# Expert pairs in twelve half phases instead of six, and the pair with the largest second expert moved from fourth to second

## The reference

```python
D_MODEL = 1024; N_EXPERTS = 8; TOP_K = 2; D_FF_EXPERT = 3584
logits = xt @ w_router + b_router
top_p, top_e = lax.top_k(softmax(logits), TOP_K)      # weights normalised to sum 1
# every expert e, for the tokens that chose it:
ye = (silu(xe @ w_gate[e]) * (xe @ w_up[e])) @ w_down[e]
# and the sum of ye * p goes back to the token's row
```

## Time and profile before

| what | value |
|---|---|
| median of 3 runs | 1355.91 us (1355.67 to 1359.97) |
| profiled execution | 1356.35 us, span 1354.6 us |
| PE busy | 1285.1 us, 95% of the span |
| expert part, first gather to last scatter | 466.39 to about 1337.7 us |
| weights over the whole program | 458.94 MB read |

### The profile page before, as it was taken

How to read it: one execution, slowest core, us unless ns; L and a number is a source line. 1 busy time by engine, 2 the same in 40 slices (tenths; PEclk the granted TensorE clock), 3 DMA queues, 4 the chain that set the end, 5 groups by cost and what they waited for, 6 DMA issues and landing times.

```text
span 1354.6 us, 28860 instructions
## 1 busy us (share of the span) xinstructions
PE 1285.1 (95%) x12945; PEld 754.5 (56%) x12946; DVE 214.9 (16%) x592; ACT 125.4 (9%) x249; POOL 19.4 (1%) x107
## 2 busy tenths in 40 slices
PE   6999999999999699999899989799999899999996
PEld 3777788877886533346533336443435466643564
DVE  0298200000005401000101000021000020101002
ACT  2200310000002310000010000010000010000002
POOL 1000000000002000000000000000000000000000
PEclk8999999999999799999999999999999999999998
DMA  9999467656436689999999999999999997799992
GB/s 332 408 403 386 163 249 238 219 177 230 166 110 250 253 302 416 419 420 421 421 419 416 418 421 420 422 418 411 418 420 422 420 398 283 266 420 357 424 397 98
DMA packets 87886, 462.25 MB, mean 341 GB/s; under 512 B 8747, under 2 KB 12119, under 8 KB 52663
## 3 DMA queue, kind: packets, MB, share of 16 engines
q1 hardware_dynamic: 86257, 458.59, 85.4%
q10 hardware_dynamic: 1494, 1.67, 0.4%
HBM read 458.94 MB, written 2.24 MB: 340 GB/s over the span
## 4 chain that ended last, share of the span: by engine, by line
PE 84%; DMA 10%; issue 2%; DVE 2%; ACT 1%; POOL 1%; SPq 0%; DVEq 0%; ACTq 0%; POOLq 0%
PE bank L1640 34%; PE bank L1378 25%; PE bank L1666 14%; DMA ring<-in_w_exp_down_dram 10%; PE bank L1569 2%; PE bank L1347 2%; PE bank L1693 1%; PE bank L1592 1%; PE bank L1335 1%; PE bank L1276 1%; PE bank L1500 0%; DVE xT L936 0%; ACT MIX L869 0%; PE bank L1514 0%; PE bank L1327 0%
## 5 line engine op out<-in xcount | busy, mean ns | idle before, releaser
L1640 PE MATMUL bank<-ring,HT 128*32 128x384 f32 (+1 forms) x5376 | 510.6, 540 | 3.6 <-DMA ring<-in_w_exp_up_dram 3.6
L1640 PEld LDWEIGHTS bank<-ring,HT 128*32 128x32 f32 x5376 | 193.1, 110 | 309.1 <-issue 267.8
L1378 PE MATMUL bank<-HT,ring 128*128 128x264 f32 x1024 | 232.9, 389 | 2.5 <-POOL HT L610 2.5
L1378 PEld LDWEIGHTS bank<-HT,ring 128*128 128x128 f32 x1024 | 194.6, 191 | 44.0 <-issue 11.1
L1666 PE MATMUL bank<-ring,hid_t 128*32 128x256 f32 x2560 | 147.8, 379 | 1.3 <-DMA ring<-in_w_exp_down_dram 1.3
L1666 PEld LDWEIGHTS bank<-ring,hid_t 128*32 128x32 f32 x2560 | 85.2, 110 | 55.7 <-issue 4.3
L1378 PE MATMUL bank<-BIG,ring 128*128 128x264 f32 x480 | 108.0, 386 | 0.0
L1666 PE MATMUL bank<-ring,COND 128*32 128x256 f32 x1568 | 91.3, 385 | 16.0 <-DMA ring<-in_w_exp_down_dram 16.0
L1378 PEld LDWEIGHTS bank<-BIG,ring 128*128 128x128 f32 x480 | 91.1, 190 | 15.5
L1211 DVE TENSOR_TENSOR MIX<-bank,MIX 128x512 f32<-128x512 f32 (+1 forms) x42 | 26.2, 625 | 399.4 <-PE bank L1640 397.6
L1666 PEld LDWEIGHTS bank<-ring,COND 128*32 128x32 f32 x1568 | 49.5, 111 | 57.1 <-DMA ring<-in_w_exp_down_dram 26.0
(11 more groups left out here) (216 smaller groups left out, 489.8 us busy)
## 6 DMA issues: line engine op xcount, KB each, us to landing
ring<-in_w_exp_gate_dram SPq DMA_DIRECT2D x64, 1024.0 KB, 22.8
ring<-in_w_exp_up_dram SPq DMA_DIRECT2D x64, 1024.0 KB, 21.5
ring<-in_w_exp_down_dram SPq DMA_DIRECT2D x64, 1024.0 KB, 26.0
ring<-in_w_ada_dram SPq DMA_DIRECT2D x48, 1024.0 KB, 11.9
ring<-in_w_exp_gate_dram SPq DMA_DIRECT2D x64, 768.0 KB, 11.7
ring<-in_w_exp_up_dram SPq DMA_DIRECT2D x64, 768.0 KB, 15.2
ring<-in_w_exp_down_dram SPq DMA_DIRECT2D x32, 1536.0 KB, 28.0
ring<-in_w_in_dram SPq DMA_DIRECT2D x10, 1024.0 KB, 25.1
```

The source lines that it names most:

```text
L1378: ins = t_.matmul(banks_of[label][:, 0:NT], w[:, k, f * P:(f + 1) * P], src(k0 + k), start=(k0 + k == 0), stop=(k0 + k == k_tiles - 1))
L1640: ins = t_.matmul(bank[banks[g]][i * GRP:(i + 1) * GRP, 0:cols], xg[:, k, c0:c0 + GRP], w[:, i, :], start=(k == 0), stop=(k == DT - 1))
```

## The change

The order of the four pairs is now ranks (0, 4), (1, 7), (2, 5), (3, 6). A pair has twelve phases instead of six: gate large, gate small, up large, up small for the first half, the same for the other half, then down large and down small for each half. Gate and up of a group now share one bank, and silu is written straight to `hidT`, in place of the buffer `sil`. SP reads the second expert's number ahead of load 8 of pair 0 (it was load 16). The tables are issued by ACT, ahead of its first wait for `flags_ready`. PE waits for bank 7 after it has read the number of passes, not before.

```diff
-RANK_AT = (0, 4, 2, 5, 3, 6, 1, 7)
+RANK_AT = (0, 4, 1, 7, 2, 5, 3, 6)
-PHASES = (("large", 0), ("small", 1), ("large", 1), ("small", 0), ("large", "down"), ("small", "down"))
+PHASES = tuple((role, kind, HALVES[role][f])
+               for kind, f in (("gate", 0), ("up", 0), ("gate", 1), ("up", 1), ("down", 0), ("down", 1)) for role in ROLES)
+DOWN_LOADS = (range(0, 8), range(8, DOWN_UNITS))
...
-                    if first and start <= RING * UNIT < start + size:
-                        spread_tables()
-                    if first and n == 2 * DT:
+                    if first and n == DT:
                         sp.wait_ge(on("flags_ready"), 1)
                         experts.append(expert_at(1))
...
-                            a.activation(sil[:, g, 0:cols], bank[GATE_BANKS[role][g]][:, 0:cols],
+                            a.activation(hidT[role, half][g], bank[GATE_BANKS[role][g]][:, 0:cols],
                                          ACT.Silu).then_inc(on(f"{role}_silu"), step_of(g, n, most))
...
+            act.wait_ge(on("pmT_ready"), 1)
+            act.dma_start(pm_rows, pmT[:]).then_inc(on("pm_rows_stored"), 16)
+            act.wait_ge(on("pm_rows_stored"), 16)
+            for i, dst in enumerate((posb, wgtb)):
+                spread = pm_rows[i * NE:(i + 1) * NE, :].rearrange("e n -> (e n)").unsqueeze(0)
+                act.dma_start(dst.rearrange("p e n -> p (e n)"),
+                              spread.to_broadcast([P, NE * NT])).then_inc(on("tables_spread"), 16)
             act.wait_ge(on("flags_ready"), 1)
...
-            for bk in range(8):
+            for bk in range(7):
                 pe.wait_ge(emptied[bk], bank_total[bk])
             pe.wait_ge(on("flags_ready"), 1)
             passes = pe.value_load(flag[0:1, 2 * NE:2 * NE + 1], min_val=1, max_val=2)
+            pe.wait_ge(emptied[7], bank_total[7])
...
-                expand("large", 0, {})
-                expand("small", 0, {3: [("large", 0, g) for g in large[:3]], 5: [("large", 0, g) for g in large[3:]]})
-                expand("large", 1, {3: small[:count["small"]]})
-                expand("small", 1, {3: [("large", 1, g) for g in large[:3]], 5: [("large", 1, g) for g in large[3:]]})
-                down("large", {4: small[count["small"]:]})
-                down("small", {})
+                early, late = (4, 7) if count["small"] == 1 else (3, 5)
+                for s in range(2):
+                    large = [("large", s, g) for g in range(count["large"])]
+                    before_it = [("small", s - 1, g) for g in range(count["small"])] if s else []
+                    expand("large", "gate", s, {3: before_it})
+                    expand("small", "gate", s, {})
+                    expand("large", "up", s, {})
+                    expand("small", "up", s, {early: large[:3], late: large[3:]})
+                down("large", 0, {4: [("small", 1, g) for g in range(count["small"])]})
+                down("small", 0, {})
+                down("large", 1, {})
+                down("small", 1, {})
```

More of the change, by code:

```diff
@@ L103, in pair_loads @@
     starts, at = [], 0
[L104 to L109, removed]
+    for role, kind, half in PHASES:
+        for i in DOWN_LOADS[half] if kind == "down" else range(DT):
+            size = DOWN_PARTS[i] * D if kind == "down" else QUAD * SPLIT[half][1]
+            starts.append((role, kind if kind == "down" else f"{kind}{half}", i, at, size))
+            at += size
     assert at % (RING * UNIT) == 0 and len(starts) == PAIR_LOADS
@@ L503, in pair_units @@
                     end = start + size
-                    if (role, kind, i) == ("large", "up1", DT - 1):
+                    if n + 1 < PAIR_LOADS and LOADS[n + 1][:3] == ("small", "gate0", 0):
                         end += LOADS[n + 1][4]
@@ L1595, in bank_free @@
                 def bank_free(role, kind, s, g):
[L1596 to L1621, removed]
-                    else:
[L1623 to L1626, removed]
@@ L1628, in expand @@
-                def expand(role, s, turns):
-                    cols, groups = SPLIT[HALVES[role][s]][1], count[role]
[L1630 to L1648, removed]
@@ L1650, in down @@
-                def down(role, turns):
-                    groups, most = count[role], MOST[role]
-                    pe.wait_ge(on(f"{role}_hidT"), p * 2 * most + 2 * most)
[L1653 to L1657, removed]
+                    most = MOST[role]
+                    if kind == "up":
+                        pe.wait_ge(on(f"{role}_silu"), p * 2 * most + (s * most + g + 1))
+                    elif s:
+                        pe.wait_ge(on(f"{role}_hidT"), p * 2 * most + (g + 1))
+                    elif role == "small":
+                        pe.wait_ge(on("x_updated"), p * DT + DT)
+                    elif g < 4:
+                        pe.wait_ge(on("xg_ready"), p * 4 + (g + 1))
+                    else:
+                        pe.wait_ge(on("x_updated"), p * DT + 5)
@@ L1658, in down @@
+                def down(role, s, turns):
+                    groups, most, half = count[role], MOST[role], HALVES[role][s]
+                    pe.wait_ge(on(f"{role}_hidT"), p * 2 * most + 2 * most)
+                    for u in DOWN_LOADS[half]:
+                        for turned in turns.get(u, ()):
+                            turn_hid(*turned)
                         parts = DOWN_PARTS[u]
                         n, w = load(parts)
+                        first, last = u == DOWN_LOADS[half][0] and not s, u == DOWN_LOADS[half][-1] and s
```

59 lines of the change are left out of this document (31 added, 28 removed).

## The result

The changed kernel takes **1348.46 us** (median of 9 runs, 1345.37 to 1349.73); the kernel before, on the same chip, 1355.91. The ratio is 0.9934, 95% interval 0.9920 to 0.9947: 9 us less (7 to 11); the medians alone differ by 7.5. The forecast was 1345.8, with 1339 to 1355 as its range. The profiled execution took 1349.01 us, its span 1347.3.

The account below looks back on a forecast made before the run. Narrow pairs were taken as load-bound at 418 GB/s, the slim one as PE-bound, coupled by the ring. Last down matmul at 1322.0 plus an unchanged 24.3 us gave 1346.2, or 1345.8 us on the median's scale; range 1339 to 1355.

Parts of the forecast that it names:

- First pair, 665.7: First narrow pair: stays load-bound and ends at 665.7 us, against 665.3 before, despite 8 MiB instead of 14 loaded ahead.
- ACT's queue, cost 0: Before the first gather: ACT's wait for the pm_rows store, landing in 1.4 us, costs nothing; 5 us later still free.
- The rival (22.6 us): First pair: pm_rows lands 22.6 to 25 us after issue, ACT delays PE, total 1359 to 1362; chance 0.12.
- its milder half: First pair: the store stands 15 us behind eight loads, costing 6 us, total 1352; within the rival's 0.12.
- The gap and the slim pair, 16.4 + 224.3: Second place: 16.4 us of gap, then the slim pair in 224.3 us without waiting, ending at 906.4.
- The lead, halving worth 10 us: Slim pair: loading ahead ends at 7.8 MiB with twelve phases, 3.7 with six; 4 MiB or 10 us difference.
- Third and fourth pair, 410.6 to 419.7: Behind the slim pair: 410.6 us by the lead, 419.7 by likeness to earlier pairs; middle taken, end at 1321.5.
- Last down matmul at 1322.0: End of the expert part: last down matmul at 1322.0 instead of 1332.1, 10.1 us less.
- small things: Slim form: waits for copies of the last two turned groups, 0.5 us in all; the rest costs nothing.
- The tail: After the last down matmul: 24.3 us to the end of the run, unchanged.
- The lead is not handed on: Rival, slim pair to pair three: loading stutters at a full ring, the 10 us gain is lost, 1356; chance 0.14.
- A fall of the clock at the end: Rival, last pair: slower clock through last loads and scatter, 15 us (chance 0.02), or scatter only, 3 to 5 (0.05).

Follow-up runs that it names:

- 2 MiB less: Changed kernel with SP writing only what would fit a ring of 12 slots, not 14: 1353.56 us, ratio 0.9966.
- third place: Slim pair third instead of second: changed kernel with twelve phases 1345.35 us, again 1344.98; kernel before with six phases 1359.21 us.

## Why the prediction was right, and where it was not

- **First pair, 665.7.** Measured 666.4. No idle loading from 465 on (419 GB/s over 465 to 475, and 419 instead of 329 over 478 to 500), the loads behind the flag issued from 462.26 on (forecast 462.5). This step held. With the tables on SP, where SP restarts as early but then stands again, the first pair ends at 670.3: an SP that does not stand is what makes up for 6 MiB less in advance. (From the two rows the matmuls take 0.108 and 0.079 us, not 0.107 and 0.080; it changes little.)
- **ACT's queue, cost 0.** The result held, the term did not: the landing was put at 1.4 us and was 6.1. The 5 us of cover absorbed it to 0.18 us. The rival (22.6 us) overstated it; its milder half, a store that stands behind eight loads for 15 us, is what happens on SP's own queue (14.5).
- **The gap and the slim pair, 16.4 + 224.3.** Measured 14.8 + 229.5, 3.6 us more. This is the term that was mis-sized: the profile of before was one of the four without a stall, and both durations were taken from it. Executions with the slow gap give 224.3 to 224.6 again. That the profile of before was of the faster kind was luck, bad luck for the number: where both have the stall, the gain is larger than the medians show (first expert matmul to last scatter 861.9 us in the kernel before with the tables moved, 850.4 in the changed one, 11.5 us less, where 10.1 had been forecast).
- **The lead, halving worth 10 us.** Six phases in the new order take 1358.4, twelve 1348.5: 9.9 us (11 by the ratios). In the windows it is 5.0 MiB where the ledger (the prediction's phase-by-phase count of the lead) had 7.8 - 3.7 = 4.1. The price of a MiB (2.5 us) is borne out by the pair behind the slim one, 12.6 us for 5.0 MiB. That 2 MiB less cost 5.1 us agrees in part by luck: 2 us of it are the first pair's, and its profile lacks the stall.
- **Third and fourth pair, 410.6 to 419.7.** Measured from 910.65 to 1325.51: 414.9, the middle (415.1). The third waited 1.9 us for loads (under 4 forecast), the fourth 9.2 (8 to 14 forecast). That the middle was hit is partly luck, since it is only the mean of two sums 9 us apart. The 14.2 us put for the gap behind the slim pair stood on no row; it measured 14.0.
- **Last down matmul at 1322.0.** Measured 1325.5: 0.7 from the first pair, 3.6 from the gap and the slim pair, less 0.2, and less the 0.5 put in for small things. The tail was 23.5 us instead of 24.3. So 1349.0 on the profile's scale, where 1346.2 was forecast.
- **The rivals.** "The lead is not handed on" describes the six phases exactly, in second and in third place, but not the twelve. A fall of the clock at the end is not seen: the granted clock is 1.00 over 1300 to 1325.5, with its waits, and 0.80 over what follows (0.78 before), which took less time than before. This core loaded at 419 GB/s over the whole third pair. The 358 GB/s per core that the Trainium skill gives (HBM Reference, Specifications) do not bind here.
- **Not seen ahead:** that third place is better. I weighed only the order that the change has. The profiles do not settle why: with a stall in both, third place is 1.1 us shorter, so most of the 3 us of the medians is not in them.

## What to carry to other kernels

When a stage bound by loads and a stage bound by compute share a ring, put the compute-bound one ahead of a load-bound one, so that its surplus is of use to somebody; but it can hand on only what the ring can hold, so first make the use of the ring even. Each of the two did nothing alone here (1.0005, 1.0017), and together 0.7%. So a change that shows no gain by itself may be half of one: look at what else caps the same quantity.

A small DMA whose landing is waited for belongs on a queue with nothing ahead of it, and its cost is to be taken from a row where that queue's neighbours are as busy as they will be.

Take a duration from more than one profile before it carries a sum of a few us: here one profile in four or so lacked a stall that the others had.

## What the runs showed of the hardware

- The same store of 16.5 KB landed in 1.4 us on an idle queue (SP's before, ACT's in the kernel before with the tables moved), in 5.2 to 6.3 us on ACT's queue while SP's eight loads were issued, and in 14.5 us on SP's queue behind them, at 418 GB/s the time of about 6 MB. The Trainium skill (DMA: Bandwidth & Descriptors, Queues, rings and completion order) has engines take turns between their queues by packets; 6 us on another queue and 14.5 on the same one agree with that.
- TensorE stood still for 2.3 to 2.7 us soon after it entered the slim form, in nine of 14 executions, for 1.2 us in a tenth, and in none of the four where the granted clock had been 0.90 in the gap ahead of it.
- One core loaded at 418 GB/s over 600 us with PE busy for 573 of them (before), and at 419 over the changed kernel's third pair with PE busy for 186.8 of 188.7.
